# Two stacks of transformer layers in one kernel: the second stack's index logits in pairs, with six products between

## What is computed

```python
h = rms_norm_2(x, g_pre_mix[l])
proj = h @ w_in[l]
u_pool, q, k, v, iq, ik, iw = jnp.split(proj, SPLIT_POINTS, axis=-1)
...
a_out = pool_mixer(u_pool, w_pool[l], pool_scale[l])
# in blocks of 64 queries:
logits = jnp.einsum('bqhd,bsd->bqhs', iqb, ik32) * (IDX_DIM ** -0.5)
score = jnp.einsum('bqh,bqhs->bqs', iwb, jax.nn.relu(logits))
score = jnp.where(allowed[None], score, -jnp.inf)
top_val, top_idx = lax.top_k(score, topk)
# then softmax attention over the picked keys
mix = jnp.concatenate([a_out, b_out], axis=-1) @ w_out[l]
```

## Time and profile before

| | us |
|---|---|
| median of 3 runs | 2510.27 (2509.81 to 2510.27) |
| the profiled execution, its time | 2509.18 |
| the profiled execution, its span | 2507.4 |
| PE busy in the span | 2398.2 (96%) |
| DVE busy in the span | 1474.6 (59%) |
| L1978 first start, last start (both layers) | 1299.2, 1942.9 |

### The profile page before, as it was taken

One profiled execution on the slowest core, in us unless ns is written; L12 is line 12 of the kernel. 1 busy time (PEld: TensorE's weight loads), 2 busy tenths in 40 slices (PEclk: granted clock), 3 DMA queues, 4 the chain that ended last, 5 costly groups with the idle time before them and its releaser, 6 DMA issues.

```text
span 2507.4 us, 28880 instructions
## 1 busy us (share of the span) xinstructions
PE 2398.2 (96%) x11342; PEld 1927.5 (77%) x11350; DVE 1474.6 (59%) x2112; ACT 832.6 (33%) x1166; POOL 366.3 (15%) x281
## 2 busy tenths in 40 slices
PE   7999999999999999999999989999989988999996
PEld 6877888888786788888867667888866866788885
DVE  6775554456686545436669856445457975643543
ACT  4554222224455422223422543222233244322221
POOL 2002000001100200000337311000024732100002
PEclk9999999999999999999999989999989998999998
DMA  4211222222221222222222111232212111122221
GB/s 154 103 58 68 101 90 95 100 101 84 100 102 44 86 101 101 85 99 101 84 72 84 51 72 68 84 104 98 100 67 89 68 55 64 67 100 102 87 97 50
DMA packets 33017, 215.53 MB, mean 86 GB/s; under 512 B 4112, under 2 KB 4368, under 8 KB 7824
## 3 DMA queue, kind: packets, MB, share of 16 engines
q1 hardware_dynamic: 32912, 214.08, 24.0%
HBM read 211.97 MB, written 2.10 MB: 85 GB/s over the span
## 4 chain that ended last, share of the span: by engine, by line
PE 79%; DVE 9%; POOL 4%; ACT 4%; issue 3%; DMA 0%; POOLq 0%; ACTq 0%; SPq 0%; DVEq 0%
PE ps L358 73%; POOL wl L339 2%; DVE wl L330 2%; ACT wh L323 1%; PE ps L471 1%; PE ps L2016 1%; DVE gl L511 1%; PE ps L2040 1%; POOL arena L1468 1%; DVE tmp L1846 1%; PE ps L1223 1%; PE ps L495 1%; PE ps L2030 1%; DVE arena L1723 1%; POOL arena L1484 1%
## 5 line engine op out<-in xcount | busy, mean ns | idle before, releaser
L358 PE MATMUL ps<-gh,wh 128*128 128x512 f32 x1504 | 598.9, 398 | 28.6 <-DVE gl L511 16.1
L358 PE MATMUL ps<-hh,wh 128*128 128x512 f32 x1504 | 598.9, 398 | 19.7 <-issue 11.5
L358 PE MATMUL ps<-gh,wl 128*128 128x512 f32 x1504 | 588.3, 391 | 0.0
L358 PE MATMUL ps<-gl,wh 128*128 128x512 f32 x1504 | 588.1, 391 | 0.0
L358 PE MATMUL ps<-hh,wl 128*128 128x512 f32 x1504 | 587.9, 391 | 0.0
L358 PE MATMUL ps<-hl,wh 128*128 128x512 f32 x1504 | 587.6, 391 | 0.0
L323 ACT ACTIVATE wh<-wr 128x2048 fp32r<-128x2048 f32 x196 | 374.0, 1909 | 554.0 <-PE ps L358 554.0
L330 DVE TENSOR_TENSOR wl<-wr,wh 128x2048 fp32r<-128x2048 f32 x176 | 406.0, 2307 | 255.8 <-ACT wh L323 255.8
L358 PEld LDWEIGHTS ps<-gh,wh 128*128 128x128 f32 x1504 | 283.0, 188 | 100.8 <-issue 17.9
L358 PEld LDWEIGHTS ps<-hh,wh 128*128 128x128 f32 x1504 | 282.9, 188 | 94.1 <-issue 25.1
L358 PEld LDWEIGHTS ps<-gl,wh 128*128 128x128 f32 x1504 | 283.3, 188 | 60.2 <-issue 2.6
(11 more groups left out here) (239 smaller groups left out, 2376.7 us busy)
## 6 DMA issues: line engine op xcount, KB each, us to landing
wr<-in_weights SPq DMA_DIRECT2D x196, 1024.0 KB, 4.8
x<-in_xt SPq DMA_DIRECT2D x4, 512.0 KB, 7.1
out_yt<-x SPq DMA_DIRECT2D x8, 256.0 KB, 2.0
arena<-in_gates SPq DMA_DIRECT2D x2, 512.0 KB, 8.0
arena<-in_embed SPq DMA_DIRECT2D x2, 512.0 KB, 5.6
par<-in_params_b SPq DMA_DIRECT2D x2, 274.0 KB, 2.7
tmp<-in_positions SPq DMA_DIRECT2D x2, 256.0 KB, 6.6
arena<-in_positions SPq DMA_DIRECT2D x2, 256.0 KB, 2.7
```

The source lines that it names most:

```text
L358: done = pe.matmul(out, stationary, moving, start=(first and n == 0), stop=(last and n == 2), skip_group_check=True)
```

## The change

Two steps of the logits are issued together, at every second k, with six products between in place of three. Steps, waits, banks and the work itself stay; only PE's order differs.

```diff
             if k >= 4:
-                logits(k - 4)
+                logit_pair(k, k - 4)
+
+        def logit_pair(k, s):
+            if k % 2 == 0:
+                logits(s)
+                logits(s + 1)
 
         product_tile(pe, mem, sem, 3, P, B_TILE[3] + 1, mem.gh, mem.gl, before=weights_and_logits)
-        product_tile(pe, mem, sem, 4, 0, B_TILE[4], mem.gh, mem.gl, before=lambda k: logits(4 + k))
+        product_tile(pe, mem, sem, 4, 0, B_TILE[4], mem.gh, mem.gl, before=lambda k: logit_pair(k, 4 + k))
         product_tile(pe, mem, sem, 4, P, B_TILE[4] + 1, mem.gh, mem.gl)
```

## The result

| | before | changed |
|---|---|---|
| median of 9 launches, us | 2510.27 (2508.08 to 2513.05) | 2515.98 (2511.46 to 2517.74) |
| ratio, 95% interval | | 1.0021 (1.0012 to 1.0030) |
| the profiled execution, time / span | 2509.18 / 2507.4 | 2511.46 / 2509.7 |

The changed kernel is 0.21% slower in this measurement, 5.3 us by the ratio; forecast were 1.9. The profiled execution, though, is only 2.3 us longer than that of before. So two things are to be explained: whether those 2.3 us are the forecast ones, and where the rest is. Together with all later launches of the same two kernels (42 of the changed one, 126 of before) the means are 2514.0 and 2510.5, +3.5 with a standard error of 0.4. The first nine launches of the changed kernel lay high (+5.6 in the mean): without them 33 launches against 117 give +3.0 (0.4).

A forecast was written before the change was run, and what follows sets the result against it. PE, busy 96%, was taken to bound the kernel, with DVE pacing the logits from 1309.96 us; per layer 0.27 + 0.68 = +0.95 us, two layers +1.9, so 2510.27 + 1.9 = 2512.2 us; 8-in-10 range 2509.6 to 2515.5.

The forecast's parts named there:

- item 2: Steps 1 to 4 of the logits: one break fewer, -0.41 us, border inside a pair free; step 4 late by +0.27.
- item 1: Step 1 directly behind step 0: starts no earlier, PE idles where three products stood; they come later, +0.68 us a layer.
- item 3: From step 4 on: ACT, DVE and POOL all move by +0.27 us with the same overlap; step 11 at 1319.75.
- items 4 and 5: Steps 5 to 11: saved breaks worth nothing, PE waits; behind step 11 six products remain instead of three, +0.68 us.
- The 0.2 at step 9: Step 9 of the logits: PE was forecast to wait about 0.2 us there, one of item 4's waits.
- It gets through to the end: Tile 9 to the attention: the whole 0.95 us a layer gets through, no cover hides it; two layers +1.9 us.
- The rule that a change of tiling mode drains TensorE: Switches between logits and products: by this rule alone six drains fewer a layer, -4.9 us; full-count rival's chance 0.04.
- The clock: Rival, behind PE's waits: one clock fall more, 2513.7, chance 0.22; two or more, 2515.2 and up, 0.10; one fewer, 0.08.

The follow-up runs named there:

- both_apart: Changed kernel with steps 0 and 1 and steps 10 and 11 apart as before, steps 2 to 9 in pairs: +1.2 (0.6) us against the kernel before.
- first_apart: Changed kernel with steps 0 and 1 apart as before, the others in pairs: +3.1 (0.9) us against the kernel before.
- last_apart: Changed kernel with steps 10 and 11 apart as before, the others in pairs: +1.3 (0.5) us against the kernel before.
- late: Kernel before with four spare products (0.91 us) ahead of tile 9 in each layer, overwritten by its first product: +3.4 (0.9) us against the kernel before.
- before_fed: Kernel before with seven spare products ahead of chunk 10, in PE's wait for POOL: +0.2 (0.8) us against the kernel before.

## Why the prediction was right in its mechanism and missed the number

- *A break costs 0.41 us, and none is inside a pair* (item 2). Right: eight records in 1.13 us for four in 0.70; both_apart gains 0.36 a layer for an expected 0.41.
- *Step 1 costs three products* (item 1). Right: 1.16 us of idle, and first_apart takes 1.02 - 0.31 = 0.71 of the passage back, for 0.68.
- *The chain moves with step 4, the contention of DVE and POOL with it* (item 3). Right: +0.27, and 8.37 us for 8.35.
- *Savings behind step 4 are waited away, and three products slip behind step 11* (items 4 and 5). Right: waits at steps 7, 10 and 11, and last_apart takes 0.70 back, for 0.68. The 0.2 at step 9 are there as well, though no row shows them as idle.
- *It gets through to the end.* Right: late, +0.93 in the second layer for four products of 0.91, and masks and v tile still end together. The waits are worth 2.03 us (traces without a fall), 1.9 were forecast.
- *The rule that a change of tiling mode drains TensorE*, which the prediction takes from the Trainium skill, "TensorEngine Tiling (Array Packing)", Key Properties. By it alone the time should have fallen by 4.9 us. The traces show that the change costs 0.41 us (whether by a drain they don't show), and not that sum: what decides is what ends the next wait.
- *The clock.* This is the step that failed. The forecast took the count of falls as unchanged and gave one more 0.22 and two more 0.10. In the passages of its six traces the changed kernel had no fall once, one once and two four times, 9 in all, or 1.5 a launch, where before had 1 in each of three. The mean sum of the two passages is 205.33 us against 202.53, +2.80, of which 2.03 are waits and 0.77 clock. I had the two kinds of place right (step 11, and POOL's wait moved), but gave one fall more a chance of 0.22 and no weight in the sum, where four of six traces had it. And I left out a place that also moves, the attention's wait of 1.85 us for DVE: there the clock fell in four of six first layers of the changed kernel and in none of before.
- *The scatter.* The number is that of nine launches, and single launches of the changed kernel range from 2510.5 to 2517.8. 42 of them have a mean 3.5 above before's; forecast 1.9, and the end of the range, 2515.5, was 5.2 above. The median of the first nine came out 5.7 above, of which about 2.5 is luck of those nine (+5.6 in the mean against +3.0 in the 33 behind them). I had made the upper end from counts of falls and left no room for scatter.

What stays open is how the clock adds up outside the passages. From the first layer's scores to step 0 of the second the six traces of the changed kernel take 522.28 to 524.54 us, in the mean 523.13, and the three of before 521.53 to 522.59, in the mean 522.15: +0.98. From the last passage to the end it is 484.2 to 484.6 against 483.3 to 484.1, +0.6. Both kernels run the same instructions there, and the fall at the attention's wait for DVE lies in the first of the two. With the passages that is +4.4, but ahead of step 0 the changed kernel's traces happen to be 0.7 shorter, and +3.7 is left between the spans. The launches say +3.0 to +3.5. So the extra over the waits, 1 to 1.5 us, is of the size that the counted falls give (0.8 in the passages, and four times in six 1.5 at the attention's wait, part of which is won back until the next layer), but no experiment took it away. Also open is what decides at which of two equal waits the clock falls. That it changes with what PE did before the wait is shown (late, and the table by place); the rule behind it isn't.

## What to carry to other kernels

Batching small work of another shape between matmuls saves the switches between the two (0.41 us each here), but only where nobody has to keep step with it. Reckon the chain of the consumers (PE, ACT, DVE and back) first: if it sets the pace, the saved time turns into idle, and what used to fill the idle is paid for behind it. And where idle stretches of PE like these (1.5 to 1.9 us) are new or move, weigh a further fall of the clock in the forecast itself, go through all such waits behind the change, and leave room in the range for the scatter of a few launches.

## What the runs showed that I had not expected

The clock of PE falls at a wait of 1.93 us in one layer and not at the same wait in the other, steadily from launch to launch (0 of 3 and 3 of 3), and in the changed kernel, where these waits come one to three microseconds later behind step 0, it is the other way round (5 of 6 and 0 of 6). It fell behind an idle of 1.54 us too, in 4 of 12 layers, with 0.6 us of idle shortly ahead, behind a wait of 1.85 us in 4 of 6 first layers and in none of before, and once at the attention's waits of 0.6 us (before_fed). A fall costs 1.5 to 1.6 us, not far from the 2.0 us that the waits of the change cost in both layers together.
